# Twenty rotary heads' projection jobs in the wide form, with the bank halves added between a job's two weight splits and the rotation behind the second

## The reference, cut to what matters

```python
h = rms_norm(x, g_mix[l])
qkv = jnp.einsum('bsd,de->bse', h, w_in[l]).reshape(bsz, seq, 3, N_MIX_HEADS, HEAD_DIM)
...
o_a = moba_attention(apply_rope(q[:, :ha], cos, sin), apply_rope(k[:, :ha], cos, sin), v[:, :ha])
o_b = stick_breaking_attention(q[:, ha:hb], k[:, ha:hb], v[:, ha:hb])
o_c = dilated_mixture(apply_rope(q[:, hb:], cos, sin), apply_rope(k[:, hb:], cos, sin), v[:, hb:])
```

```python
def apply_rope(x, cos, sin):
    x32 = x.astype(jnp.float32)
    x1, x2 = jnp.split(x32, 2, axis=-1)
    return jnp.concatenate([x1 * cos - x2 * sin, x2 * cos + x1 * sin], axis=-1).astype(x.dtype)
```

## Time and profile before

| | |
|---|---|
| median of three runs | 1193.54 us |
| the profiled execution's own time | 1193.42 us |
| its span in the trace | 1191.6 us |
| TensorE (PE) busy | 1177.9 us, 99% |
| VectorE (DVE) busy | 898.7 us, 75% |
| ScalarE (ACT) busy | 644.1 us, 54% |
| GpSimd (POOL) busy | 167.6 us, 14% |
| mean DMA rate | 189 GB/s |

### The profile page before, as it was taken

The page is one execution under the profiler, slowest core; times in us unless marked ns, Lnnn a source line. Parts: engine busy times, 40 slices in busy tenths (PEclk is TensorE's granted clock), DMA queues, the critical chain, the costliest instruction groups (busy, mean ns, idle before and its releaser), DMA issues.

```text
span 1191.6 us, 17496 instructions
## 1 busy us (share of the span) xinstructions
PE 1177.9 (99%) x6284; PEld 1014.3 (85%) x6284; DVE 898.7 (75%) x1080; ACT 644.1 (54%) x830; POOL 167.6 (14%) x169
## 2 busy tenths in 40 slices
PE   9999999999999999999999999999999999999996
PEld 7888899999988989888888888888888888888885
DVE  6658766786667967768887878878788878687764
ACT  6445545555555756655644565645465554476453
POOL 2907500030322503300000000000000000000043
PEclk9999999999999999999999999999999999999998
DMA  9664543344544444537446545646735645645631
GB/s 359 256 249 177 209 177 141 142 158 158 215 174 177 169 181 145 179 139 247 156 164 246 205 150 212 212 141 212 251 120 199 249 160 188 247 157 186 237 127 71
DMA packets 79122, 224.72 MB, mean 189 GB/s; under 512 B 3793, under 2 KB 4177, under 8 KB 68561
## 3 DMA queue, kind: packets, MB, share of 16 engines
q1 hardware_dynamic: 78336, 220.22, 51.8%
q10 hardware_dynamic: 720, 3.59, 0.8%
HBM read 221.69 MB, written 2.10 MB: 188 GB/s over the span
## 4 chain that ended last, share of the span: by engine, by line
PE 96%; DVE 1%; ACT 1%; issue 1%; DMA 1%; POOL 0%; SPq 0%; DVEq 0%; ACTq 0%
PE extra L1661 14%; PE extra L1663 14%; PE extra L1662 14%; PE banks L1414 5%; PE banks L1416 5%; PE banks L1415 5%; PE banks L1412 5%; PE banks L1409 5%; PE banks L1410 5%; PE banks L1455 3%; PE banks L1457 3%; PE banks L1456 3%; PE banks L1681 2%; PE banks L1682 2%; PE banks L1683 2%; PE extra L1683 2%
## 5 line engine op out<-in xcount | busy, mean ns | idle before, releaser
L740 ACT ACTIVATE w_high<-staged 128x1024 fp32r<-128x1024 f32 x282 | 295.3, 1058 | 250.8 <-PE extra L1663 213.4
L1198 DVE TENSOR_TENSOR w_low<-staged,w_high 128x1024 fp32r<-128x1024 f32 x282 | 342.0, 1226 | 105.0 <-ACT w_high L740 103.4
L904 DVE TENSOR_TENSOR w_low<-staged,w_high 128x1024 fp32r<-128x1024 f32 x151 | 196.7, 1307 | 91.3 <-ACT w_high L478 87.3
L478 ACT ACTIVATE w_high<-staged 128x1024 fp32r<-128x1024 f32 x144 | 151.3, 1057 | 125.7 <-PE banks L1457 47.5
L1661 PE MATMUL extra<-w_high,part_a 128*128 128x512 f32 x400 | 156.8, 392 | 0.0
L1663 PE MATMUL extra<-w_high,part_a 128*128 128x512 f32 x400 | 155.8, 389 | 0.0
L1662 PE MATMUL extra<-w_low,part_a 128*128 128x512 f32 x400 | 155.7, 389 | 0.0
L1661 PE MATMUL extra<-w_high,part_b 128*128 128x512 f32 x336 | 132.0, 393 | 0.0
L1663 PE MATMUL extra<-w_high,part_b 128*128 128x512 f32 x336 | 130.9, 390 | 0.0
L1662 PE MATMUL extra<-w_low,part_b 128*128 128x512 f32 x336 | 130.8, 389 | 0.0
L1414 PE MATMUL banks<-part_a,w_high 128*128 128x256 f32 x384 | 110.1, 287 | 0.1
(11 more groups left out here) (254 smaller groups left out, 2286.3 us busy)
## 6 DMA issues: line engine op xcount, KB each, us to landing
staged<-in_wup SPq DMA_DIRECT2D x64, 1024.0 KB, 5.1
staged<-in_wdown SPq DMA_DIRECT2D x64, 1024.0 KB, 5.1
staged<-in_wqk SPq DMA_DIRECT2D x32, 1024.0 KB, 4.8
staged<-in_wv SPq DMA_DIRECT2D x12, 1024.0 KB, 5.0
staged<-in_wbc SPq DMA_DIRECT2D x8, 1024.0 KB, 5.3
staged<-in_wmk SPq DMA_DIRECT2D x4, 1024.0 KB, 4.7
staged<-in_woa SPq DMA_DIRECT2D x4, 1024.0 KB, 4.7
staged<-in_wcq SPq DMA_DIRECT2D x4, 1024.0 KB, 4.8
```

Source lines behind the costliest of these rows:

```text
L478: nc.scalar.activation(w_high[:, job % 2, cols], staged[:, job % 4, cols], ACT.Copy).then_inc(high_ready, 1)
L740: nc.scalar.activation(half_4d(w_high, h), src, ACT.Copy).then_inc(high_ready, made)
L904: tt(w_low[:, job % 2, cols], staged[:, job % 4, cols], f32(w_high[:, job % 2, cols]), ALU.subtract).then_inc(low_ready, 1)
L1198: tt(half_4d(w_low, h), src, f32(half_4d(w_high, h)), ALU.subtract).then_inc(low_ready, made)
```

## The change

All twenty rotary jobs become wide. The bank then has two summands, which have to be added before the rotation:

- ACT: `turn` between the splits is replaced by `rope_move`, one copy of bank columns 256 to 511 into `unturned` (128 partitions by 256). `turn`, now from SBUF to SBUF, stands behind the second split, and behind the exp and ln work of the second job of a round.
- DVE: between the splits stands `rope_sum`, which adds bank columns 0 to 255 to `unturned` and frees the bank. The three instructions of `roped` stand behind the second split, ahead of the attention work of the round.
- `rope_move` waits for the rotation before (`rotated`), since `unturned` is one buffer.

```diff
-            def turn(off, job, n_out):
+            def rope_move(off, job, n_turn):
 
                 act.wait_ge(half_done, off(2) + (2 * job + 2))
-                act.wait_ge(taken, off(1) + (BANKS + n_out))
-                src = bank[job % 4]
-                nc.scalar.activation(spare[0:64, 0, :], src[64:P, 0:T], ACT.Copy)
-                nc.scalar.activation(spare[64:P, 0, :], src[0:64, 0:T], ACT.Copy).then_inc(turned, 1)
+                act.wait_ge(rotated, off(1) + (n_turn + 1))
+                nc.scalar.activation(unturned, bank[job % 4][:, T:2 * T], ACT.Copy).then_inc(rope_moved, 1)
+
+            def turn(off, n_out):
+
+                act.wait_ge(taken, off(1) + (BANKS + n_out + 1))
+                nc.scalar.activation(swapped[0:64, :], unturned[64:P, :], ACT.Copy)
+                nc.scalar.activation(swapped[64:P, :], unturned[0:64, :], ACT.Copy).then_inc(turned, 1)
...
-            def roped(off, slot, n_turn, n_out, job):
+            def rope_sum(off, n_turn, job):
 
                 done(off, job)
-                src = bank[job % 4]
+                dve.wait_ge(rope_moved, off(1) + (n_turn + 1))
+                tt(unturned, unturned, bank[job % 4][:, 0:T], ALU.add).then_inc(taken, 1)
+
+            def roped(off, slot, n_turn):
 
                 dve.wait_ge(turned, off(1) + (n_turn + 1))
-                tt(spare[:, 1, :], src[:, 0:T], rope[:, 0, :], ALU.mult).then_inc(rope_made, 1)
-                tt(spare[:, 0, :], spare[:, 0, :], rope[:, 1, :], ALU.mult).then_inc(rope_made, 1)
+                tt(unturned, unturned, rope[:, 0, :], ALU.mult).then_inc(rope_made, 1)
+                tt(swapped, swapped, rope[:, 1, :], ALU.mult).then_inc(rope_made, 1)
                 dve.wait_ge(rope_made, off(2) + (2 * n_turn + 2))
-                tt(slot, spare[:, 0, :], spare[:, 1, :], ALU.add).then_inc(taken, 1)
+                tt(slot, swapped, unturned, ALU.add).then_inc(rotated, 1)
...
                 for s in range(4):
                     split(by(i), JOB_C + s + 2, 0)
-                    roped(by(i), qk[:, i * 4 + (SLOT_C + s), :], s, OUT_C + s, JOB_C + s)
+                    rope_sum(by(i), s, JOB_C + s)
                     split(by(i), JOB_C + s + 2, 1)
+                    roped(by(i), qk[:, i * 4 + (SLOT_C + s), :], s)
...
-                    job_of(by(i), JOB_C + s, OUT_C + s, part_a, wide=False)
+                    job_of(by(i), JOB_C + s, OUT_C + s, part_a)
```

More of the change, by code:

```diff
@@ L125, in build @@
         spare, squares = quad[:, 0:2, :], quad[:, 2:4, :]
+        unturned, swapped = quad[:, 0, :], quad[:, 3, :]
         acc = sb("acc", [P, T])
@@ L202, in build @@
         rope_ready, v_scaled = sem("rope_ready"), sem("v_scaled")
-        turned, rope_made = sem("turned"), sem("rope_made")
+        rope_moved, turned, rope_made, rotated = sem("rope_moved"), sem("turned"), sem("rope_made"), sem("rotated")
         held_ready, s_ready, t_ready, o_ready, o_taken = (
@@ L578, in _ @@
                     split(by(i), JOB_C + s + 2, 0)
-                    turn(by(i), JOB_C + s, OUT_C + s)
+                    rope_move(by(i), JOB_C + s, s)
                     if s == 1:
@@ L588, in _ @@
                     split(by(i), JOB_C + s + 2, 1)
+                    turn(by(i), OUT_C + s)
                 act.wait_ge(o_ready, i + 2)
@@ L601, in _ @@
                     split(by(i), JOB_A + s + 2, 0)
-                    turn(by(i), JOB_A + s, OUT_A + s)
+                    rope_move(by(i), JOB_A + s, 2 * HEADS_C + s)
                     if s == 1:
@@ L609, in _ @@
                     split(by(i), JOB_A + s + 2, 1)
+                    turn(by(i), OUT_A + s)
                 act.wait_ge(o_ready, i + 5)
@@ L944, in _ @@
             dve.sem_inc(taken, BANKS)
+            dve.sem_inc(rotated, 1)
             for t in range(KT):
@@ L1021, in _ @@
                             tt(score[h], score[h], extra[2 + h][:, 0:CAUSAL], ALU.subtract).then_inc(logw_ready, 1)
-            dve.wait_ge(taken, BANKS + OUT_A)
+            dve.wait_ge(rotated, 1 + 2 * HEADS_C)
             with dve.Fori(0, HEADS_A // 2) as i:
@@ L1031, in _ @@
                     split(by(i), JOB_A + s + 2, 0)
-                    roped(by(i), qk[:, i * 8 + slot_a(s), :], 2 * HEADS_C + s, OUT_A + s, JOB_A + s)
+                    rope_sum(by(i), 2 * HEADS_C + s, JOB_A + s)
                     split(by(i), JOB_A + s + 2, 1)
+                    roped(by(i), qk[:, i * 8 + slot_a(s), :], 2 * HEADS_C + s)
                     if s == 0:
@@ L1076, in group_a @@
                     nc.vector.reciprocal(total[:, 0:4], total[:, 0:4]).then_inc(inv_a, 1)
-            dve.wait_ge(taken, BANKS + OUT_MK)
+            dve.wait_ge(rotated, 1 + 2 * HEADS_C + 2 * HEADS_A)
             for s in range(4):
@@ L1537, in _ @@
                 for s in range(4):
-                    job_of(by(i), JOB_A + s, OUT_A + s, part_a, wide=False)
+                    job_of(by(i), JOB_A + s, OUT_A + s, part_a)
                     if s == 0:
@@ L1563, in group_a @@
                     pe.wait_ge(o_taken, 1 + HEADS_B + MIX_C + 2 * i)
+                    pe.wait_ge(rotated, 1 + 2 * HEADS_C + 4 * (i + 1))
                     for h in range(2):
```

## The result

The changed kernel takes 1194.9 us (median of 22 runs, 1194.26 to 1197.21), the kernel before on the same chips 1193.5 us (22 runs, 1193.02 to 1194.09). The ratio is 1.0013, with an interval of 1.0007 to 1.0019: 1.4 us slower. That is inside the 0.2% that the prediction calls no change, but the interval leaves out 1, so the loss is real. The forecast was 1194.3 us, with a range of 1192.0 to 1196.7.

A forecast was written before the change was run, and what follows sets the result against it. TensorE, busy in 99% of the span, was taken to bound the kernel. Against the profiled 1193.42 us, -3.9 + 2.2 + 1.9 + 0.6 = +0.8 gave 1194.2, and 1194.3 for the median; range 1192.0 to 1196.7.

The forecast's parts named there:

- The waits: TensorE stands for DVE's later work: C loop 0.74 us a round, 2.2 in all; A loop 0.94 more, twice, 1.9.
- The saving: Wide rotary jobs on TensorE take 5.57 us instead of 5.77: 0.20 us a job, 3.9 us for twenty.
- The head of the A loop: TensorE waits once, 0.6 us (ends 0 and 1.3), for DVE's copies ahead of the A loop's first scores.
- a rotation beside POOL: Head of the A loop: DVE's rotation running beside POOL's squaring was taken to add 0.7 us, between 0 and 1.4.
- the saving would arrive whole: Rival: chains shorter than read, or TensorE need not stand behind DVE's rotation; 1189.6 us, chance 0.06.
- only the A loop would hold TensorE: Rival: in the C loop some 0.7 us of the chain is covered; 1192.1 us, chance 0.10.
- The slower rival: POOL and DVE exclude each other at the head of the A loop: +4.1 us, 1197.6 us, chance 0.12.
- The price that the rival gave: Rival: TensorE's clock falls in the new waits; 5.57 us more a job, five jobs 28 us: 1222, chance 0.02.

The follow-up runs named there:

- e1: Changed kernel with DVE's rotation behind the attention work of the job instead of ahead of it, in both loops; 1190.29 us, ratio 0.9970 to the kernel before.
- e3: Kernel before with only DVE's rotation moved behind the second split, narrow jobs and ACT's half copies kept; 1200.45 us, ratio 1.0058.
- e8: Changed kernel with POOL's six squares and sums for group B's norm left out, a one-column memset standing for each; 1194.48 us, ratio 1.0006.
- e4: Changed kernel with ACT's half copies and DVE's rotation put back between the two splits, behind the new sum; 1200.28 us, ratio 1.0056.
- e6: e4 with POOL's six squares held until the third rotation of the first A round is finished; 1198.11 us, ratio 1.0041 to the kernel before.
- e5: Changed kernel with POOL's six squares for group B's norm held until the third rotation of the first A round is finished; 1195.65 us, ratio 1.0021.

## Why the prediction was right

**The waits.** This step carried the forecast. The wait in the C loop was predicted as 0.74 us from the start that TensorE could have had, and is 0.72; the growth of the wait in the A loop was to be 0.94, and is 1.21 - 0.29 = 0.92. The chain was shortened on ACT by 0.51 and lengthened on DVE by 1.25, as said: `soft` starts 5.69 us behind job 1's end, where 4.97 + 0.74 = 5.71 stood. e1 shows that the rotation's place is the cause, with nothing on ACT changed, and e3 shows it from the other side.

**The saving** was mis-sized: 0.20 us a job, 3.9 in all, against 0.18 and 3.6 measured (e1's rounds). The 5.77 us of a narrow job were read from one start to the start of the sums; 48 starts at 0.12 us are 5.76, so 0.01 to 0.02 us of the passage to another kind of matmul were counted as saving, and twenty of them make the 0.3 us.

**The restart behind a wait** was missing from the sum: 0.11 us each time, three times in the C loop and once at the first scores. With the saving this is why the C loop came out at +0.32 us where the prediction's terms give 12 x -0.20 + 2.2 = -0.2. In the A loop they give -1.6 + 1.9 + 0.6 = +0.9, and +0.98 is measured. Over both loops the terms gave +0.8 us and the traces +1.3: the saving set 0.3 too high and the restarts left out are most of that gap.

**The head of the A loop** was right in kind and high in size: TensorE starts there 0.39 us late (253.44 - 246.16 = 7.28 against 7.07 - 0.18), with 0.1 of restart behind it, where 0.6 stood. That these lie so near is in part luck, for the reasons are another mix. The copies were expected at 4.75 us behind job 3 and start at 4.63, but of the 0.7 us that I took for a rotation beside POOL only 0.2 came (L929 at 0.60), since POOL's start moved too (3.29 instead of 2.81), by ACT's half copies ahead of the outputs. In its place stood 0.34 us in which DVE waits for its own rotation, a wait that was not in my sum; e8, without POOL, has it as well. The copies then took 2.4 us instead of 2.7 (250.79 to 253.17), and TensorE started 0.27 us behind them, not 0.05. e8 shows POOL's part of this: with it gone no wait for the copies is left. By the Trainium skill ("SBUF — State Buffer", section "Who interferes with whom") a DVE instruction with two inputs from SBUF contends with a POOL instruction that reads SBUF, a copy can do so when it runs in a mode that uses two ports, and a reduction never does. The traces agree: products take 0.83 us beside POOL against 0.42, copies 1.65 against 0.69, while the peaks take 1.41 us in the kernel before with POOL at work throughout (from 258.61) and 1.41 in e8 without it.

**The rivals.** That the saving would arrive whole, or only the A loop would hold TensorE, failed at the three waits of the C loop. The slower rival, POOL against DVE over a whole round, did not decide here, but it exists: in e4 the first round lost 3.22 us, and e6 moves that loss by moving POOL. What keeps it small in the changed kernel is that ACT's half copies stand behind exp. Even so it was close: DVE's peaks and ACT's exp, which needs them, in the first A round:

```profile
260.21 1.41 DVE L1054 TENSOR_REDUCE peak<-x 128x1 f32<-128x384 f32 x2
```
```profile
261.66 0.61 ACT L612 ACTIVATE x<-x,peak 128x384 f32<-128x384 f32 x1
```

The peaks end at 261.62, 0.04 us before exp starts, and exp starts where ACT's own copy (261.38) lets it. More than 0.04 us of further delay on DVE would have held it up; the prediction had found a margin of some 0.5 there. In e8, without POOL, the peaks end 1.1 us ahead of exp.

The clock stayed up behind the waits of up to 1.2 us in the profiled execution of the changed kernel, and e4 shows that it falls behind longer ones. But one of the 22 executions, the slowest (1197.21 us), has a mean granted clock of 0.995, as the profiled one of e6 has, where the other 21 have 0.997 or 0.998; e5 has one such in eleven (1197.6 us). There is no trace of either, so whether the clock fell behind one of these waits stays open. The price that the rival gave was far above the falls that were seen: one costs 1.7 us in e4 and in e6, where 5.57 a job for five jobs had been reckoned.

**The version that beats both** is e1: the change with the rotation one step further back, 1190.29 us, 3.4 less than the kernel before beside it.

## What to carry to other kernels

Where an engine is full and its neighbours are not, read for each thing that it waits for how late it may come, and compare that with what a change puts ahead of it; here 0.2 us of slack in the C loop met 0.74 us of added chain, and a saving of 3.6 us on the full engine became a loss of 1.4. When work moves past a point for which it is not needed, move it past everything that something waits for, not only past the instruction that stood in the way. Delaying an engine that disturbs another only moves the disturbance, unless it finds a stretch in which nobody waits: POOL's eleven microseconds cost no less in the second round than in the first.

## What the runs showed of the hardware

- TensorE's granted clock is 1.00 behind waits of 1.2 us (changed kernel), 1.55 us (e3) and 1.59 us (e6, first A round). It fell to 0.50, the level of 1.2 GHz, behind 2.08 us (e6) and 3.22 us (e4), for some 3.4 us, and each fall cost 1.7 us beyond the wait. In e4 it fell only some 1.1 us after the matmuls had begun again. In e6 it fell in the profiled execution; the mean clocks of the other four speak against a fall in them. I had given the clock 0.02 as a rival, for waits of at most 1.4 us, and had not carried it into what I expected of e4.
- The first matmul pair behind a wait of TensorE takes 0.33 us to the next start, and without a wait 0.22 (the sums of the changed kernel and of e1). Each such wait costs 0.11 us beyond its own length.
- Behind a copy on ACT from PSUM over 128 partitions by 256 the next instruction starts after 0.28 us; behind one of the copies of 64 partitions that swap halves after 0.40 from PSUM (177.54 to 178.34 for two) and 0.43 from SBUF (264.75 to 265.18 in e4). A copy of half the data occupies ACT longer here; no run tells whether that comes from the swap.
